# The opening of a three-layer stack: each entered group of channels feeds its chunk of three weight blocks instead of one

## The chip, the cores and the metric

One core of one Trainium2 chip runs the whole program. The metric is the device time of one execution in microseconds (us), taken as the median of the runs; lower is better.

## The reference, cut to what matters

Two hybrid layers and one further layer work on 256 tokens of 2048 channels. Only the start of the first layer is touched by the change:

```
mod = dot(silu(c), w_ada) + b_ada          # c: 2048; w_ada: 2048 x 6144
shift, scale, gate = split(mod, 3)
u = rms_norm(x, norm_w) * (1 + scale) + shift
proj = dot(u, w_in)                        # w_in: 2048 x 19064
... iq (index queries, 1024 columns), dk and dv (keys and values, 512),
    ik, iw, dt, f (128 columns, "misc"), dq (1024), and the rest
```

So the first product with w_in can start only when shift and scale are known for a group of channels, and these are themselves sums over 16 MB each of w_ada.

## The kernel before, in words

**Numbers.** All operands are f32. Every product with w_in is made of three products of rounded pieces: the weights are split into HH (ScalarE, `hi`, L1455) and LL (VectorE, `lo`, L1812, written in place over RAW), u into UH and UL. A *chunk* is 1 MB of weights: four k-tiles of 128 rows by 512 columns. With 256 tokens in two halves that is 24 matmuls of 128x512 (L1214), each `gemm`. Four chunks make a *block* of 512 output columns, which ends in two PSUM banks. Blocks alternate between two pairs of banks (`set`, G0/G1 and G2/G3).

**Order.** A planner (`Order`) writes one list of steps; each engine's program is the list's steps of its kind, in that order, with semaphores between engines. An engine thus never passes a step that waits. After each `gemm` comes a `slot`: one step of a lane `side` (attention, index scores, scan work, rope tables) and one of a lane `evac` (what follows a finished block). Lanes are first in, first out. All weights are fetched by the SP queue (L1069), in the order of the list, and each fetch first waits until the last reader of its buffer is done (L1066).

**The opening** (`open`, the first layer only). The 2048 channels enter in four groups of four 128-channel tiles. For one group, eight sums over the 2048 inputs of w_ada are needed: four for scale, four for shift. Each sum reads 1 MB. Six are made on VectorE (`dot`, L1805, one pass over 128x2048 with a running sum), two on TensorE (L1231, 16 products with one moving column, 32 matmuls in the trace; `ON_PE = 2`). The order in a group is: shift 2 on TensorE, scale 0 and 1, shift 3 on TensorE, scale 2 and 3, then the fetch and `hi` of the group's chunk of the first index query block, shift 0 and 1. Then `am` (L1897 to L1902) adds the biases, `u` scales and shifts the group's channels (ScalarE L1504 and L1509, VectorE L1954), and `lo` and `gemm` of that chunk follow directly. The sums use six fetch buffers in turn (0 to 5), the chunks two (6 and 7).

**The first x.** x is loaded, squared (ScalarE L1447), scaled by its root (L1468, two halves one after the other) and turned by TensorE through the banks BA and BC (L1246, L1459) within the first group.

**After the opening** one chunk is multiplied per slot: the last of iq0, then misc, iq1, dkv, dq0, dq1, the convolution blocks (from chunk 21 on) and so on. Five buffers serve them, and sums for the second layer (`ada`, 1 MB each, L1823) are woven in at two per five chunks until the convolution blocks. `misc_work` runs in seven slots once misc is done, and index scores, the first attention and the scan follow it on the side lane. In every block of heads (`heads`) the two token halves are copied, rotated and turned in slots of their own, through bank BE. The rope tables are side steps of the opening's slots.

Of the kernel before, what the change touches and what calls it, by code (L numbers as in the profile page):

```python
# [32 lines left out]

ON_PE = 2

# [69 lines left out]
class Order:  # L105
# [3 lines left out]
    def __init__(self):  # L109
        self.plan = []  # L110
        self.evac, self.side = Lane(), Lane()
        self.packed = {}
        dots = list(range(NR + NX - 2))

        self.ring, self.buf_user = {"dot_dve": dots, "dot_pe": dots, "all": [NR + NX - 2, NR + NX - 1]}, {}
        self.fetches = []
        self.chunks = []
        self.blocks = []
        self.pend = []
        self.evac_last, self.side_last = ("start",), ("start",)  # L120
        self.evac_before, self.side_before = {}, {}
        self.user = [None, None]
        self.ada = {"list": [], "i": 0, "job": None, "every": 0, "count": 0, "next": 0, "got": []}
        self.ada_info, self.cb, self.dots = [], [], {}
# [100 lines left out]
    def begin(self, chunks, evac, x, ready, kts, needs=None, after=None, soon=None):  # L225
        b = {"n": len(self.blocks), "set": len(self.blocks) % 2, "x": x, "ready": ready, "kts": kts, "evac": evac, "chunks": chunks,
             "needs": needs or (lambda k0: []), "after": after, "soon": soon, "job": None, "free_by": None, "end": None}
# [86 lines left out]

    def open(self, block, between, enter):


        for gi in range(4):
            dots = [("scale", m, "dve") for m in range(4)] + [("shift", m, "dve") for m in range(4 - ON_PE)]
            for i, m in zip((0, 3), range(4 - ON_PE, 4)):  # L320
                dots.insert(i, ("shift", m, "pe"))
            for i, (kind, m, engine) in enumerate(dots):
                if i == 6:
                    self.bring(block["chunks"][gi])
                self.dot(kind, 4 * gi + m, engine)
                between(gi, i)
            enter(gi)
            if gi < 3:
                self.put("lo", block["chunks"][gi]["g"])
                self.gemm(block["chunks"][gi])  # L330
                self.slot()
        self.pend.append(block["chunks"][3])
        self.ring = {"all": sorted(range(NR), key=lambda i: self.buf_user[i])}


def work_order():
# [23 lines left out]

    def heads(h):
        def steps(b):
            o.head_block[h] = b
# [122 lines left out]

    def enter_first(gi):
        put("am", 0, gi)
        put("u", 0, gi)
        ended("u_lo", 0, 2 * gi + 1)  # L490
# [32 lines left out]

    o.head_block, o.tok_block, o.freed = {}, {}, {}

# [122 lines left out]
    put("start")  # L648
    for gen in (load_layer(0), rope(0), rope(1)):
        o.side.add(gen)  # L650
# [4 lines left out]
    for l in range(2):  # L655
# [10 lines left out]
        if l == 0:  # L666
            first = o.wblock(w, IQ, heads(("iq", 0, 0)), u_ready, kind="tm", begun=True)
            o.open(first, first_x, enter_first)
            o.ada["list"] += [(1, part, pair, half) for half in range(2) for part in range(2) for pair in range(8)]
            o.ada["every"] = (2, 5)  # L670
            iq_b = [first]
        else:
            iq_b = [o.wblock(w, IQ, heads(("iq", l, 0)), u_ready, kind="tm", needs=u_needs, soon=(lambda e=entered: e))]
        misc_b = o.block([one], misc(l), ("U", 0), u_ready, KT)
        iq_b.append(o.wblock(w, IQ + 512, heads(("iq", l, 1)), u_ready, kind="tm"))
        o.side.add(o.when([misc_b], misc_work(l)))
        o.side.add(o.when(iq_b, index_scores(l)))
        dkv_b = o.wblock(w, DK, heads(("dk", l, 0)), u_ready, kind="tm")
        dq_b = [o.wblock(w, DQ + j * 512, heads(("dq", l, j)), u_ready, kind="tm") for j in range(2)]
# [84 lines left out]
def hybrid_stack(nc, A, out):  # L764
# [181 lines left out]
    x_turned, x_put = count("x_turned", o.all("x_in")), count("x_put", o.all("x_in"))  # L946
    x_sum, x_normed = count("x_sum", o.all("x_norm")), count("x_normed", o.all("x_norm"))
    rope_ang = count("rope_ang", o.all("rope"))
# [93 lines left out]
    def tokens_of(b, t):  # L1042

        return (gemm_done if t else tm_half).at(o.blocks[b]["last"])

    def freed(key):
# [131 lines left out]
    def tensor_program(pe):  # L1178
# [60 lines left out]
        def x_in(c):  # L1239
            bk = (BA, BC)[c % 2]  # L1240
            pe.wait_ge(*x_normed.at(1))
            if c >= 2:
# [32 lines left out]
        def hd_turn(h, t):  # L1275
            weight, rot, n = HEADS[h[0]]
            pe.wait_ge(*(hd_rot if rot else hd_scaled).at(h, t))
            pe.wait_ge(*(hd_put.at(h, 0) if t else evac_before("hd", h, 0)))
            for c in range(n):
                mm = pe.transpose(BE[:, c * P:(c + 1) * P], SS[t][:, c * P:(c + 1) * P], ident)  # L1280
            mm.then_inc(*hd_turned.up(h, t))
# [150 lines left out]
    def scalar_program(a):  # L1432
# [30 lines left out]

        def x_norm(t):
            a.wait_ge(*x_sum.at(t))
            rstd(0, t, SSQ[:, t:t + 1])
            a.wait_ge(*rstd_done.at(0, t))
            a.activation(kv2[:, t, :], kv2[:, t, :], ACT.Copy, scale=RST[:, t:t + 1]).then_inc(*x_normed.up(t))  # L1468

# [65 lines left out]
        def hd_store(h, t):  # L1535
            weight, rot, n = HEADS[h[0]]
            dst, first = head_dst[h[0]](h[2])
            scale = {"fq": PB[:, 120:121], "fk": PB[:, 121:122], "dq": HD_SCALE, "q2": HD_SCALE}
            a.wait_ge(*hd_turned.at(h, t))
            a.activation(dst[:, first:first + n, t * P:(t + 1) * P], BE[:, 0:n * P].rearrange("p (a b) -> p a b", a=n),  # L1540
                         ACT.Copy, scale=scale[h[0]] if h[0] in scale else 1.0).then_inc(*hd_put.up(h, t))
# [242 lines left out]
    def vector_program(v):  # L1784
# [96 lines left out]

        def x_norm(t):
            rstd(0, t)

# [595 lines left out]
```

## Time and profile before

| what | value |
|---|---|
| median of 3 runs | 3477.04 us (3476.33 to 3477.14) |
| profiled execution, its own time | 3473.09 us |
| its span | 3471.3 us |
| TensorE busy | 3335.0 us, 96% of the span |
| VectorE busy | 2238.9 us, 64% |
| ScalarE busy | 1701.7 us, 49% |
| moved by DMA | 719.32 MB, 207 GB/s over the span |

The profile is one execution. A busy engine is one whose instructions are running; TensorE's granted clock is given beside it in tenths of full speed or as a share. The trace is counted in us from the start of the span.

### The profile page before, as it was taken

How to read it: one execution, taken by the hardware profiler on the slowest of the kernel's cores; microseconds unless marked ns; L12 is line 12 of the kernel's file. 1: busy time of each engine (PE TensorE's matmuls, PEld its weight loads, DVE VectorE, ACT ScalarE, POOL GpSimd, SP SyncE). 2: the span in 40 equal slices, each digit the busy share in tenths (PEclk: the TensorE clock that was granted, in tenths of full speed). 3: DMA queues.
4: the chain of work that ended last, by engine and by line, in shares of the span. 5: the costliest groups of instructions: out<-in, count | busy, mean ns of one | idle time of the engine just before them, and what ended most of it. 6: DMA issues, size and time to landing. Idle time of an engine off the chain costs nothing.

```text
span 3471.3 us, 43913 instructions
## 1 busy us (share of the span) xinstructions
PE 3335.0 (96%) x18250; PEld 2894.8 (83%) x18250; DVE 2238.9 (64%) x2687; ACT 1701.7 (49%) x2098; POOL 46.8 (1%) x90
## 2 busy tenths in 40 slices
PE   5799989989999999999999999999999999999998
PEld 4679978878888887799788878888888899988887
DVE  5688777866666556687666576655567776544544
ACT  3354565554434344546655544343446875434343
POOL 0000000000000000000000000000000000000000
PEclk8799999999999999999999999999999999999999
DMA  8654456556677655444544467765555443455554
GB/s 354 261 222 173 170 209 248 219 199 249 260 279 287 224 183 193 162 179 158 180 172 159 174 234 267 272 249 196 189 183 191 177 173 140 158 218 194 194 184 156
DMA packets 102918, 719.32 MB, mean 207 GB/s; under 512 B 12176, under 2 KB 12256, under 8 KB 18752
## 3 DMA queue, kind: packets, MB, share of 16 engines
q1 hardware_dynamic: 93888, 675.38, 52.5%
q0 software_dynamic: 8256, 37.64, 3.1%
q8 instruction: 144, 2.36, 0.3%
q10 hardware_dynamic: 576, 3.50, 0.3%
q14 instruction: 54, 0.44, 0.0%
HBM read 710.08 MB, written 6.40 MB: 206 GB/s over the span
## 4 chain that ended last, share of the span: by engine, by line
PE 86%; DVE 7%; ACT 3%; DMA 2%; issue 1%; SPq 0%; DVEq 0%; ACTq 0%
PE G L1214 79%; DVE LL L1812 3%; DMA RAW<-w_ada_turned_packed_dram 1%; PE BA L1362 1%; PE BD L1335 1%; DVE S L2019 1%; PE BD L1397 1%; DMA RAW<-in_w_in_packed_dram 1%; ACT HH L1455 1%; PE BC L1348 0%; DVE RAW L1823 0%; PE BE L1280 0%; PE BA L1416 0%; PE BC L1416 0%; PE BC L1380 0%
## 5 line engine op out<-in xcount | busy, mean ns | idle before, releaser
L1455 ACT ACTIVATE HH<-RAW 128x2048 fp32r<-128x2048 f32 x546 | 1044.7, 1914 | 1138.1 <-PE G L1214 838.4
L1812 DVE TENSOR_TENSOR LL<-RAW,HH 128x2048 fp32r<-128x2048 f32 x546 | 1247.8, 2287 | 357.8 <-ACT HH L1455 357.3
L1214 PE MATMUL G<-HH,UH 128*128 128x512 f32 x2560 | 1022.1, 399 | 61.2 <-DVE LL L1812 57.2
L1214 PE MATMUL G<-LL,UH 128*128 128x512 f32 x2560 | 1003.6, 392 | 0.0
L1214 PE MATMUL G<-HH,UL 128*128 128x512 f32 x2560 | 1003.3, 392 | 0.0
L1214 PEld LDWEIGHTS G<-HH,UH 128*128 128x128 f32 x2560 | 485.1, 189 | 171.0 <-DVE LL L1812 67.4
L1214 PE MATMUL G<-UH,HH 128*128 128x256 f32 x2080 | 602.9, 290 | 9.8 <-DVE XS L2055 7.2
L1214 PE MATMUL G<-UH,LL 128*128 128x256 f32 x2080 | 589.2, 283 | 0.0
L1214 PE MATMUL G<-UL,HH 128*128 128x256 f32 x2080 | 588.9, 283 | 0.0
L1214 PEld LDWEIGHTS G<-LL,UH 128*128 128x128 f32 x2560 | 484.5, 189 | 103.7
L1214 PEld LDWEIGHTS G<-HH,UL 128*128 128x128 f32 x2560 | 485.6, 190 | 100.6 <-issue 2.9
L1214 PEld LDWEIGHTS G<-UH,HH 128*128 128x128 f32 x2080 | 399.4, 192 | 15.7 <-DVE LL L1812 12.5
L1214 PEld LDWEIGHTS G<-UL,HH 128*128 128x128 f32 x2080 | 399.5, 192 | 2.0 <-issue 1.0
L1214 PEld LDWEIGHTS G<-UH,LL 128*128 128x128 f32 x2080 | 399.1, 192 | 0.0
L1214 PE MATMUL G<-HH,YH 128*128 128x512 f32 x768 | 299.9, 391 | 3.0 <-DVE LL L1812 3.0
L1214 PE MATMUL G<-LL,YH 128*128 128x512 f32 x768 | 298.9, 389 | 0.0
L1214 PE MATMUL G<-HH,YL 128*128 128x512 f32 x768 | 298.8, 389 | 0.0
L1214 PEld LDWEIGHTS G<-HH,YH 128*128 128x128 f32 x768 | 144.2, 188 | 33.6 <-DVE LL L1812 3.9
L1214 PEld LDWEIGHTS G<-LL,YH 128*128 128x128 f32 x768 | 144.1, 188 | 30.3
L1214 PEld LDWEIGHTS G<-HH,YL 128*128 128x128 f32 x768 | 144.2, 188 | 29.4
L1823 DVE SCALAR_TENSOR_TENSOR RAW<-RAW,CH 128x1024 f32<-128x1024 f32 x128 | 151.4, 1220 | 11.5 <-DMA RAW<-w_ada_turned_packed_dram 11.5
L2019 DVE SCALAR_TENSOR_TENSOR S<-G,PAR,S 128x253 f32<-128x253 f32 x144 | 69.3, 481 | 52.1 <-ACT S L1571 48.3
(336 smaller groups left out, 2304.2 us busy)
## 6 DMA issues: line engine op xcount, KB each, us to landing
RAW<-in_w_in_packed_dram SPq DMA_DIRECT2D x402, 1024.0 KB, 4.8
RAW<-w_ada_turned_packed_dram SPq DMA_DIRECT2D x88, 1024.0 KB, 4.9
RAW<-in_w_out_packed_dram SPq DMA_DIRECT2D x48, 1024.0 KB, 4.8
RAW<-in_w_o_ssd_packed_dram SPq DMA_DIRECT2D x32, 1024.0 KB, 4.8
RAW<-in_w_o_fox_packed_dram SPq DMA_DIRECT2D x16, 1024.0 KB, 4.8
RAW<-in_w_o_dsa_packed_dram SPq DMA_DIRECT2D x16, 1024.0 KB, 4.9
RAW<-in_w_proj_a_packed_dram SPq DMA_DIRECT2D x16, 1024.0 KB, 4.8
RAW<-in_w_proj_b_packed_dram SPq DMA_DIRECT2D x16, 1024.0 KB, 4.8
```

The lines of the kernel that those rows point to most:

```text
L1214: mm = pe.matmul(to, lt, rh, start=first, stop=end, skip_group_check=True)
L1335: mm = pe.matmul(BD[:, j * P:(j + 1) * P], vt[:, t, vof(h + j):vof(h + j) + P], W[3][:, (j * nt + t) * P:(j * nt + t + 1) * P], start=t == ...
L1362: mm = pe.matmul(to, QQ[:, h + j, qt * P:(qt + 1) * P], kt[:, kof(h + j), 0:nk], start=True, stop=True)
L1397: pe.matmul(BD[:, j * 64:(j + 1) * 64], W[j // 4][:, (j % 4) * P:(j % 4 + 1) * P], XD[:, j * 64:(j + 1) * 64], start=True, stop=True)
L1455: a.activation(HH[g % NH][:, :n], RAW[buf(ch["f"])][:, :n], ACT.Copy).then_inc(*hi_done.up(g))
L1812: v.tensor_tensor(LL[buf(f)][:, :n], RAW[buf(f)][:, :n], HH[g % NH][:, :n].bitcast(F32), ALU.subtract).then_inc(*lo_done.up(g))
L1823: done = v.scalar_tensor_tensor(r, r, 0.5, CH[:, :], ALU.mult, ALU.mult, accum_out=DOT[:, e["half"], c:c + 1])
L2019: v.scalar_tensor_tensor(to, of, weight(j), to, ALU.mult, ALU.add).then_inc(*done.up(*key, n))
```

## The change

The opening now serves three blocks: both index query blocks and the keys and values. Each group of channels brings three chunks. In the order of a group, the chunks' fetches stand before shift 0, shift 1 and the TensorE sum; one sum is on TensorE and seven on VectorE. `u` and the three products of a group are no longer at its end but inside the next group: `u` and two chunks after scale 1, the third chunk after scale 3. The sums use four buffers (5, 6, 7, 0), the chunks four (1 to 4). The third block's sums are kept in the banks BA and BC. The first rope table is made ahead of the opening, x is normed earlier and with one semaphore, and the three blocks' heads are worked off with both token halves in one slot, turned through BE and BD. The misc block comes after the three.

```diff
-ON_PE = 2
+ON_PE = 1
+DOT_BUFS, CHUNK_BUFS = [5, 6, 7, 0], [1, 2, 3, 4]
...
-        dots = list(range(NR + NX - 2))
-        self.ring, self.buf_user = {"dot_dve": dots, "dot_pe": dots, "all": [NR + NX - 2, NR + NX - 1]}, {}
+        dots = list(DOT_BUFS)
+        self.ring, self.buf_user = {"dot_dve": dots, "dot_pe": dots, "all": list(CHUNK_BUFS)}, {}
...
-    def open(self, block, between, enter):
+    def open(self, blocks, between, am, u):
+        def chunk(gi, n):
+            return blocks[n]["chunks"][gi]
+        def multiply(gi, ns):
+            for n in ns:
+                self.put("lo", chunk(gi, n)["g"])
+                self.gemm(chunk(gi, n))
+                self.slot()
         for gi in range(4):
             dots = [("scale", m, "dve") for m in range(4)] + [("shift", m, "dve") for m in range(4 - ON_PE)]
-            for i, m in zip((0, 3), range(4 - ON_PE, 4)):
-                dots.insert(i, ("shift", m, "pe"))
+            for m in range(4 - ON_PE, 4):
+                dots.insert(6, ("shift", m, "pe"))
             for i, (kind, m, engine) in enumerate(dots):
-                if i == 6:
-                    self.bring(block["chunks"][gi])
+                if 4 <= i < 7:
+                    self.bring(chunk(gi, i - 4))
                 self.dot(kind, 4 * gi + m, engine)
                 between(gi, i)
-            enter(gi)
-            if gi < 3:
-                self.put("lo", block["chunks"][gi]["g"])
-                self.gemm(block["chunks"][gi])
-                self.slot()
-        self.pend.append(block["chunks"][3])
+                if gi and i == 1:
+                    u(gi - 1)
+                    multiply(gi - 1, (0, 1))
+                elif gi and i == 3:
+                    multiply(gi - 1, (2,))
+            am(gi)
+        u(3)
+        multiply(3, (0,))
+        self.put("lo", chunk(3, 1)["g"])
+        self.pend += [chunk(3, 1), chunk(3, 2)]
...
     def first_x(gi, i):
-        if gi == 0 and i == 4:
-            put("x_norm", 0)
-            put("x_norm", 1)
-        if gi == 0 and i == 5:
+        if gi == 0 and i == 1:
+            put("x_norm")
+        if gi == 0 and i == 3:
             for c in range(KT // 2):
                 put("x_in", c)
...
-    def heads(h):
+    def heads(h, two_banks=False):
+        def at_once(b):
+            o.head_block[h] = b
+            o.two_banks.add(h)
+            for t in range(2):
+                put("hd", h, t)
+            o.blocks[b]["free_by"] = ("hd_scaled" if HEADS[h[0]][0] else "hd_copied", h, 1)
+            yield
+            for t in range(2):
+                put("hd_turn", h, t)
+            ended("hd_put", h, 1)
...
     put("start")
-    for gen in (load_layer(0), rope(0), rope(1)):
+    for part in range(2):
+        put("rope", 0, part)
+    for gen in (load_layer(0), rope(1)):
         o.side.add(gen)
...
-            first = o.wblock(w, IQ, heads(("iq", 0, 0)), u_ready, kind="tm", begun=True)
-            o.open(first, first_x, enter_first)
+            iq_b = [o.wblock(w, IQ + j * 512, heads(("iq", 0, j), True), u_ready, kind="tm", begun=True) for j in range(2)]
+            dkv_b = o.wblock(w, DK, heads(("dk", 0, 0), True), u_ready, kind="tm", begun=True)
+            o.open(iq_b + [dkv_b], first_x, am_first, u_first)
...
+    GB.append([BA, BC])
```

## Rows read from the trace of the kernel before

**Rows 1.** Busy by stretch: PE, PEld, DVE, ACT, POOL, clock, DMA share, GB/s.

```profile
0.00:134.00 134.00, 74.38 (x360) 67.92 (x360) 76.76 (x103) 42.49 (x54) 3.56 (x10) 0.75 0.86 346
134.00:212.00 78.00, 74.36 (x342) 60.85 (x343) 58.07 (x101) 40.36 (x52) 1.09 (x2) 0.95 0.52 193
212.00:430.00 218.00, 215.69 (x1592) 201.73 (x1591) 171.41 (x300) 117.06 (x208) 1.10 (x2) 1.00 0.50 184
430.00:480.00 50.00, 41.06 (x180) 32.53 (x179) 31.85 (x42) 31.61 (x70) 1.06 (x2) 0.93 0.62 232
480.00:700.00 220.00, 216.79 (x1235) 187.74 (x1234) 172.42 (x233) 119.90 (x201) 3.17 (x6) 0.99 0.60 223
```

**Rows 2.** What the SP queue waited for, 0 to 150 us: total, times, longest.

```profile
SPq L1069 <- PE BE L1231: 48.0, 4, 20.2
SPq L1069 <- PE BD L1231: 42.9, 4, 17.7
```

**Rows 3.** Chain that ended last, 0 to 160 us: start, us, what.

```profile
57.01 4.09 PE BE L1231 x32
61.12 0.33 SPq L1069
61.49 7.07 DMA RAW<-w_ada_turned_packed_dram
68.58 2.31 DVE RAW L1805 x2
...
77.72 8.48 PE G L1214 x24
...
106.12 7.95 PE G L1214 x24
...
134.19 13.35 PE G L1214 x72
```

**Rows 4.** VectorE in order of time: start, us; waits in brackets.

```profile
16.47 2.29 DVE L1805 SCALAR_TENSOR_TENSOR RAW<-RAW,CB 128x2048 f32<-128x2048 f32 x1 [6.67 <-DMA RAW<-w_ada_turned_packed_dram]
...
66.06 2.29 DVE L1805 SCALAR_TENSOR_TENSOR RAW<-RAW,CB 128x2048 f32<-128x2048 f32 x1 [7.33 <-DMA RAW<-w_ada_turned_packed_dram]
...
106.71 0.26 DVE L1868 SCALAR_TENSOR_TENSOR WW<-WW 128x96 f32<-128x96 f32 x1
...
127.48 0.16 DVE L1897 TENSOR_TENSOR AM<-DOT,MOD 128x4 f32<-128x4 f32 x1
...
130.64 1.29 DVE L1954 TENSOR_TENSOR UL<-S,UH 128x512 fp32r<-128x512 f32 x2 [2.66 <-ACT UH L1509]
131.85 4.48 DVE L1812 TENSOR_TENSOR LL<-RAW,HH 128x2048 fp32r<-128x2048 f32 x2
...
141.73 2.29 DVE L1812 TENSOR_TENSOR LL<-RAW,HH 128x2048 fp32r<-128x2048 f32 x1
```

**Rows 5.** ScalarE in order of time, same columns.

```profile
19.28 1.91 ACT L1447 ACTIVATE XS<-KV 128x2048 f32<-128x2048 f32 x1 [0.69 <-DMA KV<-in_x_dram]
...
140.31 0.58 ACT L1533 ACTIVATE S<-G 128x512 f32<-128x512 f32 x1
...
199.17 1.92 ACT L1455 ACTIVATE HH<-RAW 128x2048 fp32r<-128x2048 f32 x1 [5.05 <-DMA RAW<-in_w_in_packed_dram]
201.11 1.28 ACT L1684 ACT_TABLE_LOAD   x1
```

**Rows 6.** TensorE in order of time: sums before warm-up and after.

```profile
25.38 6.99 PE L1231 MATMUL BD<-CT,RAW 128*128 128x1 f32 x32 [6.98 <-DMA RAW<-in_w_ada_packed_dram]
...
86.05 9.68 PE L1231 MATMUL BD<-CT,RAW 128*128 128x1 f32 x64
```

**Rows 7.** Chain that ended last, 180 to 235 us: start, us, what.

```profile
183.35 10.95 PE G L1214 x48
...
211.56 8.45 PE G L1214 x36
```

**Rows 8.** DMA rate in 40 equal slices of 0 to 134 us.

```profile
GB/s 147 393 259 432 408 418 418 423 423 421 421 423 423 421 423 418 86 0 120 423 406 320 423 421 428 279 5 318 423 421 428 430 426 372 2 198 423 399 374 428
```

More of the change, by code:

```diff
@@ L225, in begin @@
     def begin(self, chunks, evac, x, ready, kts, needs=None, after=None, soon=None):
-        b = {"n": len(self.blocks), "set": len(self.blocks) % 2, "x": x, "ready": ready, "kts": kts, "evac": evac, "chunks": chunks,
+        n = len(self.blocks)
+        b = {"n": n, "set": n if n < 3 else (n - 3) % 2, "x": x, "ready": ready, "kts": kts, "evac": evac, "chunks": chunks,
              "needs": needs or (lambda k0: []), "after": after, "soon": soon, "job": None, "free_by": None, "end": None}
@@ L359, in rope @@
         side_ended("rope_sin", r, 1)
-    def heads(h):
+    def heads(h, two_banks=False):
[9 more added lines that the diff above has]
+            ended("hd_put", h, 1)
         def steps(b):
+            if two_banks:
+                yield from at_once(b)
+                return
             o.head_block[h] = b
@@ L522, in out_layer @@
                 o.evac.add(modulated(l + 1))
-    o.head_block, o.tok_block, o.freed = {}, {}, {}
+    o.head_block, o.tok_block, o.freed, o.two_banks = {}, {}, {}, set()
     def load_layer(which):
@@ L666, in work_order @@
         if l == 0:
-            first = o.wblock(w, IQ, heads(("iq", 0, 0)), u_ready, kind="tm", begun=True)
-            o.open(first, first_x, enter_first)
+            iq_b = [o.wblock(w, IQ + j * 512, heads(("iq", 0, j), True), u_ready, kind="tm", begun=True) for j in range(2)]
+            dkv_b = o.wblock(w, DK, heads(("dk", 0, 0), True), u_ready, kind="tm", begun=True)
+            o.open(iq_b + [dkv_b], first_x, am_first, u_first)
             o.ada["list"] += [(1, part, pair, half) for half in range(2) for part in range(2) for pair in range(8)]
             o.ada["every"] = (2, 5)
-            iq_b = [first]
+            misc_b = o.block([one], misc(l), ("U", 0), u_ready, KT)
         else:
             iq_b = [o.wblock(w, IQ, heads(("iq", l, 0)), u_ready, kind="tm", needs=u_needs, soon=(lambda e=entered: e))]
-        misc_b = o.block([one], misc(l), ("U", 0), u_ready, KT)
-        iq_b.append(o.wblock(w, IQ + 512, heads(("iq", l, 1)), u_ready, kind="tm"))
+            misc_b = o.block([one], misc(l), ("U", 0), u_ready, KT)
+            iq_b.append(o.wblock(w, IQ + 512, heads(("iq", l, 1)), u_ready, kind="tm"))
         o.side.add(o.when([misc_b], misc_work(l)))
         o.side.add(o.when(iq_b, index_scores(l)))
-        dkv_b = o.wblock(w, DK, heads(("dk", l, 0)), u_ready, kind="tm")
+        if l:
+            dkv_b = o.wblock(w, DK, heads(("dk", l, 0)), u_ready, kind="tm")
         dq_b = [o.wblock(w, DQ + j * 512, heads(("dq", l, j)), u_ready, kind="tm") for j in range(2)]
@@ L1044, in tokens_of, with turn_bank @@
         return (gemm_done if t else tm_half).at(o.blocks[b]["last"])
+    def turn_bank(h, t):
+        return BD if t and h in o.two_banks else BE
     def freed(key):
@@ L1277, in hd_turn @@
             pe.wait_ge(*(hd_rot if rot else hd_scaled).at(h, t))
-            pe.wait_ge(*(hd_put.at(h, 0) if t else evac_before("hd", h, 0)))
+            pe.wait_ge(*(hd_put.at(h, 0) if t and h not in o.two_banks else evac_before("hd", h, 0)))
             for c in range(n):
-                mm = pe.transpose(BE[:, c * P:(c + 1) * P], SS[t][:, c * P:(c + 1) * P], ident)
+                mm = pe.transpose(turn_bank(h, t)[:, c * P:(c + 1) * P], SS[t][:, c * P:(c + 1) * P], ident)
             mm.then_inc(*hd_turned.up(h, t))
@@ L1462, in rstd, with x_norm @@
             a.activation(RST[:, t:t + 1], sq, ACT.Sqrt, bias=EPT[:, 0:1], scale=1.0 / D).then_inc(*rstd_root.up(n, t))
[L1464 to L1468, printed above, removed]
+        def x_norm():
+            for t in range(2):
+                a.wait_ge(*x_sum.at(t))
+                rstd(0, t, SSQ[:, t:t + 1])
+            for t in range(2):
+                a.wait_ge(*rstd_done.at(0, t))
+                i = a.activation(kv2[:, t, :], kv2[:, t, :], ACT.Copy, scale=RST[:, t:t + 1])
+            i.then_inc(*x_normed.up())
         def norm(n, t):
@@ L1880, in rstd, with x_norm @@
             v.reciprocal(RST[:, t:t + 1], RST[:, t:t + 1]).then_inc(*rstd_done.up(n, t))
-        def x_norm(t):
-            rstd(0, t)
+        def x_norm():
+            for t in range(2):
+                rstd(0, t)
         def norm(n, t):
```

12 lines of the change are left out of this document (7 added, 5 removed).

## The prediction, made before the changed kernel ran

> **What bounds the kernel now.** I read the busy time by stretch first. Outside the opening TensorE is all but full: 215.7 of 218 us between 212 and 430, 216.8 of 220 between 480 and 700. In the first 134 us it is busy 74.4, at a mean clock of 0.75, and most of that is not products with w_in [rows 1]. So a product that moves from behind the opening into its holes is won, as long as the opening does not grow by as much.
>
> Then what paces the opening. The SP queue waits 91 us for TensorE's sums, eight times [rows 2], and the DMA rate falls from about 421 GB/s to nothing once in each group [rows 8]. The chain shows one turn: a TensorE sum ends at 61.1, SP issues, a transfer lands, a VectorE sum ends at 70.9, ScalarE scales the channels, and the group's product starts at 77.7; the next two start at 106.1 and 134.2 [rows 3]. A turn is 28.2 us. Neither DMA nor VectorE fills it.
>
> **Prices.** 1 MB (1.049 MB in bytes) at 421 GB/s is 2.5 us [rows 8]. A fetch issued into an idle queue at 61.12 is used at 66.06, 4.9 us later, and the next at 68.56, 2.5 after it [rows 3, 4]. Two `lo` in sequence take 4.5 us, and a sum lasts as long, so each is 2.2 [rows 4]. A warm chunk is 10.95 / 2 = 5.5 us [rows 7]. A chunk after an idle stretch is 8.5 and 8.0 us, and less before shorter waits [rows 3]: I take 7.9. From `am` to the first product is 134.19 - 127.48 = 6.7 us [rows 3, 4]. A TensorE sum is 7.0 us at the 1.2 GHz level [rows 6] and 4.1 just after a chunk [rows 3].
>
> **What is removed and what is added.** At 134.19 the kernel before has nine chunks of these three blocks and misc still to multiply. After the changed opening only three and misc remain, so 6 x 5.5 = 33 us leave the full stretch. The opening gets eight more fetches, four more sums and six more `lo` steps on VectorE (22 us together), and four TensorE sums fewer, worth 16 to 28 us of PE time that lay under waits.
>
> If only the sum of work counted, a group would need 11 fetches x 2.5 = 27.4 us of DMA; VectorE 7 x 2.2 + 3 x 2.2 + 1.3 + 0.7 = 24; TensorE 7.9 + 11 + 4 = 23. All under the present 28.2. But the buffers join them into a ring. The four chunk buffers serve three chunks per group, so chunk 1 of group g goes where chunk 0 of group g-1 was, and chunk 2 where chunk 1 of g-1 was; the reader is the product. In SP's order the TensorE sum's and the last VectorE sum's fetches stand behind chunk 2. Hence this turn, from the end of product 1 of group g-1 (call it 0):
>
> chunk 2 issued 0, lands 4.9; TensorE sum's data 7.4; last VectorE sum's data 9.9; summed 12.2; `am` 12.9; two sums of the next group (they stand before `u` on VectorE, and cover the 2.7 that it now waits there for ScalarE [rows 4]) 17.3; UL 18.6; `lo` 20.8; product 0, cold, 28.7; product 1, 34.2.
>
> That is 34.2 us a turn in place of 28.2. The TensorE sum is covered: product 2 runs from 0 to 5.5, the sum from 7.4 to about 12, while VectorE waits until 12.2. If product 2 is late, or the sum runs at 7.0, it ends at 14.4 and `am` waits 2.2 more.
>
> **The first group.** The first rope table stands ahead of the first sum. Its second half waits for ScalarE, which first squares x until 21.3 [rows 5]; with a table load of 1.3 [rows 5], a sine of some 0.3 and five VectorE steps of 0.26 behind it [rows 4], the first sum starts at about 24.2 instead of 16.5 [rows 4]. It frees buffer 5 at 26.5, and the sixth fetch goes out then; five are in the queue, the fifth landing at about 27.9, so little of DMA is lost. From there each transfer follows at 2.5: shift 0 31.4, chunk 1 33.9, shift 1 36.4, chunk 2 38.9, TensorE's 41.4, the last 43.9; summed 46.2, `am` 46.9. The data of the next two sums land at 46.4 and 48.9 and end by 51.3; UL 52.6, `lo` 54.8. Product 0 54.9 to 62.8, product 1 to 68.3. x is ready before that: it is scaled right after the second sum (28.6), two passes of 2, and turned in 7, so by 40.
>
> Two turns more: 68.3 + 68.4 = 136.7. From there the fourth group's last sum ends 12.2 later (148.9), and 6.9 after that its first product starts: **155.8 us, against 134.2 before: 21.6 later**.
>
> **To the common point.** The two orders meet at the start of chunk 15 (third chunk of dq0), which before is 211.6, the product behind a stall [rows 7]. After: chunk 9 cold 7.9; then a new hole, because both halves of the first heads stand before `lo` of chunk 10 on VectorE and the second half can only be copied when chunk 9 is through: from the copy at 140.31 to the next `lo` at 141.73 it is 1.4 now [rows 4, 5], and with `lo` 2.2 and the handovers 3.8; chunks 10, 11, 13, 14 22; misc 5.8; turning heads 2.3. Together 41.8, so 197.6: 14 us earlier. The fetches are early enough, each buffer being freed some 12 us before its chunk is due.
>
> The 14 us hold something that may come back. Before 211.6, TensorE waits 10 us: a chunk lands at 199.2, after ScalarE waited 5.1 for it, and behind its `hi` come the misc chain, three table loads and the second half of the keys' heads [rows 5, 7]. In the new order misc follows eight chunks later, among the first convolution blocks, where no `ada` fetches hold up the ring (the 5 us for the landing chunk), but the chain is the same. Ends: nothing and 10 us. I take 5, for the half that was not the landing. So 9 us are left.
>
> The side lane behind it (index scores, first attention) moves by eight slots too. Convolution blocks carry it at 99% of TensorE [rows 1], so losing it there wins nothing; on the head blocks it meets square roots. These blocks lose 3.2 us in 220 when the scan shares them, but 8.9 in 50 where its first unit meets two halves of heads [rows 1]. The first unit of the scan moves off the first head block, so I set this at zero, between -6 and +18. The `ada` sums that drop out of the shortened stretch (about three) move to later blocks where TensorE is full and VectorE has room: nothing. The changed bank sets and semaphores of x: nothing, under the same waits.
>
> **Sum.** +21.6 for the opening, -35.6 from there to chunk 15 (77.4 becomes 41.8), +5: **-9 us**. Against the profiled execution, 3471.3 of span and 3473.1 of time, that is 3462 and 3464; the median lies 3.9 above that time, so 3468.
>
> One rule speaks to the DMA price. The Trainium skill, "DMA: Bandwidth & Descriptors", section "Where 436 GB/s comes from", holds that loads from HBM are bound by about 358 GB/s per core, not by the fabric's 435. [Rows 8] show 418 to 430 GB/s for tens of us, so the measurement decides against it here. By the rule, 1 MB would be 2.9 us, a turn would be 35.1 and the opening some 3 us longer, an estimate from that page.
>
> **The rivals.**
>
> A, the forecast: the turn is paced by the two products that free the chunk buffers. -9, with 3460 to 3475 as its own range. Half.
>
> B, DMA paces the groups: if the product's end is early enough, a group is 27.4 us, 6.8 less in each of two turns, -9 - 14 = -23, so 3454. For it: DMA runs unbroken whenever SP is free [rows 8]. Against it: SP must wait for the product by its own order. 0.15.
>
> C, no change to be measured: the misc stall comes back whole (+5) and the TensorE sum runs at the lower level in each group, 2.2 x 3 = +6.6, since those sums let the clock fall even now (9.7 us for two [rows 6]). +3, so 3480; with one of them alone 3473 to 3475. 0.2.
>
> D, slower: the first attention lands on the four halves of the fq heads. ScalarE changes its table for each, at 1.28 [rows 5], and TensorE waits as between 430 and 480, 8.9 us for two halves [rows 1]: 18 for four, -9 + 18 = +9, so 3486. It decides for slower from 16 us on. Against it: the scan does the same beside the fk heads and little is lost. 0.15.
>
> **How the numbers follow.** 0.2%, 7 us, is what can be told from no change. Of A's half, 0.36 falls beyond 7 us and 0.14 within; B adds 0.15 to faster, C 0.2 to the same, D 0.15 to slower. Faster 0.51, same 0.34, slower 0.15. The range takes in A, B and C and the lower edge of D: 3454 to 3484.
>
> **What would show it.** Right: the first products of the four groups' chunk 0 start at about 55, 89, 123 and 156; SP waits for L1214, not for L1231; a product's end, then an issue, in the chain; TensorE idle some 10 us per group before product 0, and the clock low at its start; a hole of about 4 us after chunk 9; chunk 15 near 198. Wrong: a start of the fourth group at 142 (B); TensorE's sum as the last to end before `am` (C); idle time on TensorE between 380 and 480 above that of before (D). The prediction falls if the opening is off by more than 6 us, or if holes behind chunk 15 are more than 10 us larger or smaller.

## The result and the profile after

| | before | changed |
|---|---|---|
| median of the runs | 3476.68 us (4 runs, 3471.77 to 3477.14) | 3453.69 us (4 runs, 3453.29 to 3454.94) |
| span of the profiled execution | 3471.3 us | 3451.8 us |
| TensorE busy | 3335.0 us | 3314.4 us |

The ratio is 0.9939, with a 95% interval from 0.9927 to 0.995. By the medians the kernel became 23 us faster (17 to 25 by the interval); 9 had been forecast. The first line of the changed kernel's page:

```profile
PE 3314.4 (96%) x18122; PEld 2876.5 (83%) x18122; DVE 2248.8 (65%) x2695; ACT 1698.0 (49%) x2096; POOL 46.8 (1%) x90
```

**The opening after.** The chain of the changed kernel (start, us, what), which answers to [rows 3]:

```profile
56.66 13.42 PE G L1255 x48
70.10 0.33 SPq L1110
70.47 6.86 DMA RAW<-in_w_ada_packed_dram
77.38 5.96 PE BE L1272 x32
83.71 4.42 DVE RAW L1850 x4
...
91.59 13.06 PE G L1255 x48
...
126.66 12.64 PE G L1255 x48
139.32 0.33 SPq L1110
139.70 8.49 DMA RAW<-in_w_ada_packed_dram
148.23 7.00 PE BE L1272 x32
...
161.82 8.28 PE G L1255 x24
...
173.90 7.37 PE G L1255 x24
```

L1255 is the product (L1214 before) and L1272 the sum on TensorE. The groups' first products start at 56.7, 91.6, 126.7 and 161.8; about 55, 89, 123 and 156 had been forecast. Each turn is two products, the issue that their end allows, a transfer, and then TensorE's own sum. SyncE's waits from 0 to 150 (waited for, us, times, longest), which answer to [rows 2]:

```profile
SPq L1110 <- PE G L1255: 52.6, 6, 13.3
SPq L1110 <- DVE RAW L1850: 42.7, 12, 22.0
SPq L1110 <- PE BD L1272: 18.3, 2, 9.3
SPq L1110 <- PE BE L1272: 6.6, 1, 6.6
```

The queue that waited 91 us for TensorE's sums now waits 25 for them and 53 for the products. VectorE's timeline in the last group (start, us, instruction, idle before and its releaser) shows the sum ending last:

```profile
155.26 0.16 DVE L1946 TENSOR_TENSOR SH<-BE,MOD 128x1 f32<-128x1 f32 x1 [1.89 <-PE BE L1272]
```

**By stretch.** Columns as in [rows 1]; the changed kernel:

```profile
0.00:162.00 162.00, 88.33 (x377) 75.65 (x378) 104.64 (x135) 56.47 (x63) 3.56 (x10) 0.78 0.80 319
162.00:194.00 32.00, 28.19 (x136) 23.76 (x137) 16.11 (x24) 8.92 (x10) 0.00 (x0) 0.86 0.36 129
194.00:212.00 18.00, 18.00 (x84) 14.91 (x83) 10.32 (x23) 10.73 (x21) 0.00 (x0) 1.00 0.66 238
212.00:430.00 218.00, 214.30 (x1567) 199.95 (x1567) 180.45 (x318) 122.78 (x221) 2.20 (x4) 1.00 0.50 180
430.00:480.00 50.00, 46.61 (x234) 38.15 (x233) 34.27 (x43) 32.75 (x65) 0.53 (x1) 1.00 0.58 219
```

To 194, TensorE is idle for 73.7 and 3.8 us, 77.5 in all; from 194 to 212 not at all. In the next two it is idle for 3.7 and 3.4 us. It was 2.3 and 8.9 in the kernel before [rows 1], where the second is the stretch with the scan's first unit and two halves of heads: rival D's collision did not come.

**A fairer common point.** Chunk 15, which the prediction used, is not preceded by the same work in both kernels, and as it turned out the stall ahead of it was misread. The start of chunk 13 is cleaner: both kernels have then multiplied the three blocks and misc. It is 194.12 before and 194.01 after. In 194 us the opening and its three blocks have won 0.1. The same view of the kernel before, around that point:

```profile
134.19:194.20 60.01, 60.00 (x285) 49.76 (x286) 45.52 (x71) 29.82 (x35) 0.00 (x0) 0.97 0.52 195
194.20:211.56 17.36, 13.92 (x57) 10.69 (x55) 11.93 (x27) 9.91 (x17) 1.09 (x2) 0.90 0.49 185
```

Where the starts of some later chunks lie (us), and what each stretch gave:

| start of | before | changed | won in the stretch |
|---|---|---|---|
| chunk 13 | 194.12 | 194.01 | 0.1 |
| convolution blocks (21) | 251.80 | 240.06 | 11.6 |
| fq blocks | 411.32 | 399.34 | 0.2 |
| gates behind fv | 582.65 | 565.15 | 5.5 |
| sz blocks | 635.95 | 619.64 | -1.2 |
| second gates | 753.18 | 731.61 | 5.3 |
| third branch product | 860.91 | 840.07 | -0.7 |
| end of the span | 3471.3 | 3451.8 | -1.3 |

The table's 11.6 is in part TensorE work of the side lane that now comes after the start of the convolution blocks (run 8 shows it), so a single row is rough; the sum is not. So 19.4 of the 19.5 us lie behind the point at which the changed part of the program is over. Idle time says the same. Before chunk 13 TensorE is idle 59.8 us before (134.19 less the 74.4 busy of [rows 1], and nothing from there) and 77.5 after: 17.7 more. Its busy time there shrank by about as much, from 134.3 to 116.5, since half of its sums are gone. Over the whole span idle time grew by only 1.1 (3471.3 less 3335.0 is 136.3, and 3451.8 less 3314.4 is 137.4), so behind that point 16.6 us of holes have closed. The two stretches in which most closed, of the kernel before and then of the changed one:

```profile
411.32:582.65 171.33, 158.71 (x734) 128.53 (x732) 128.05 (x160) 100.01 (x190) 3.71 (x7) 0.97 0.59 224
635.95:753.18 117.23, 105.44 (x502) 87.18 (x501) 84.93 (x120) 67.36 (x95) 0.00 (x0) 0.95 0.58 215
```

```profile
399.34:565.15 165.81, 161.63 (x799) 133.55 (x798) 129.30 (x172) 105.47 (x215) 3.18 (x6) 1.00 0.61 227
619.64:731.61 111.97, 104.47 (x515) 87.00 (x513) 90.06 (x136) 69.27 (x103) 0.00 (x0) 1.00 0.59 216
```

Idle there: 12.6 and 11.8 before, 4.2 and 7.5 after; 3.4 more closed from 194.20 to 211.56, 16.1 together. The same blocks are multiplied in these stretches. They became 5.5 and 5.3 us shorter. The first won less than its idle time lost, since TensorE also does more in it (799 matmuls for 734, 2.9 us): work of the side lane has moved there. TensorE's waits in the first of them, before and then after:

```profile
PE G L1214 <- DVE LL L1812: 6.1, 5, 1.5
PE BE L1280 <- DVE S L1976: 5.7, 3, 3.0
```

```profile
PE G L1255 <- DVE LL L1857: 2.6, 2, 1.5
```

L1280 turns a half of heads and waits for VectorE's rotation or scaling of it. Those waits are gone.

### The profile page after: what moved, and what is told of

It is laid out like the page before. It is cut to its first block, busy times and chain, and to the rows that moved or that the text cites. A ratio compares the mean times of both kernels' runs of the same rounds, so it can differ in the third digit from the quotient of the medians.

```text
span 3451.8 us, 43659 instructions
## 1 busy us (share of the span) xinstructions
PE 3314.4 (96%) x18122; PEld 2876.5 (83%) x18122; DVE 2248.8 (65%) x2695; ACT 1698.0 (49%) x2096; POOL 46.8 (1%) x90
## 4 chain that ended last, share of the span: by engine, by line
PE 86%; DVE 8%; ACT 3%; DMA 2%; issue 1%; DVEq 0%; ACTq 0%; SPq 0%
PE G L1255 79%; DVE LL L1857 3%; DMA RAW<-in_w_ada_packed_dram 1%; PE BA L1403 1%; PE BD L1376 1%; PE BD L1438 1%; DVE S L2065 1%; ACT HH L1496 1%; DVE RAW L1850 1%; DVE RAW L1868 1%; DMA KV<-in_x_dram 0%; PE BC L1389 0%; PE BA L1457 0%; PE BC L1457 0%; PE BD L1272 0%
## 5 line engine op out<-in xcount | busy, mean ns | idle before, releaser
L1255 PE MATMUL G<-HH,UH 128*128 128x512 f32 x2528 | 1006.1, 398 | 48.8 <-DVE LL L1857 44.2
L1255 PE MATMUL G<-LL,UH 128*128 128x512 f32 x2528 | 989.0, 391 | 0.0
L1255 PE MATMUL G<-HH,UL 128*128 128x512 f32 x2528 | 988.7, 391 | 0.0
L1255 PE MATMUL G<-UH,HH 128*128 128x256 f32 x2080 | 604.5, 291 | 12.1 <-DVE XS L2101 8.2
L1255 PEld LDWEIGHTS G<-HH,UH 128*128 128x128 f32 x2528 | 477.7, 189 | 154.4 <-DVE LL L1857 52.2
L1255 PE MATMUL G<-UH,LL 128*128 128x256 f32 x2080 | 590.6, 284 | 0.0
L1255 PE MATMUL G<-UL,HH 128*128 128x256 f32 x2080 | 590.6, 284 | 0.0
L1255 PEld LDWEIGHTS G<-LL,UH 128*128 128x128 f32 x2528 | 477.2, 189 | 101.5
L1255 PEld LDWEIGHTS G<-HH,UL 128*128 128x128 f32 x2528 | 477.9, 189 | 98.6 <-issue 2.6
L1255 PEld LDWEIGHTS G<-UH,HH 128*128 128x128 f32 x2080 | 400.9, 193 | 19.5 <-DVE LL L1857 15.0
L1255 PEld LDWEIGHTS G<-UL,HH 128*128 128x128 f32 x2080 | 401.2, 193 | 2.1 <-issue 1.2
L1255 PEld LDWEIGHTS G<-UH,LL 128*128 128x128 f32 x2080 | 400.9, 193 | 0.0
L1255 PE MATMUL G<-HH,YH 128*128 128x512 f32 x768 | 300.6, 391 | 2.8 <-DVE LL L1857 2.8
L1255 PE MATMUL G<-LL,YH 128*128 128x512 f32 x768 | 299.6, 390 | 0.0
L1255 PE MATMUL G<-HH,YL 128*128 128x512 f32 x768 | 299.5, 390 | 0.0
L1255 PEld LDWEIGHTS G<-HH,YH 128*128 128x128 f32 x768 | 144.6, 188 | 33.6 <-DVE LL L1857 3.7
L1255 PEld LDWEIGHTS G<-LL,YH 128*128 128x128 f32 x768 | 144.6, 188 | 30.2
L1255 PEld LDWEIGHTS G<-HH,YL 128*128 128x128 f32 x768 | 144.5, 188 | 29.7
```

Source lines behind the costliest of these rows:

```text
L1255: mm = pe.matmul(to, lt, rh, start=first, stop=end, skip_group_check=True)
```

## The experiments: the opening

Every kernel here computes the whole reference. Ratios are to the kernel before on the same chip. The intervals of runs 1 to 5 overlap with that of the changed kernel (0.9927 to 0.995), so of these runs the starts in the trace, one execution each, say more than the medians; that of run 6 does not overlap.

**1. Five chunk buffers.** If the products pace a turn by freeing the chunk buffers, a fifth buffer shortens it; if DMA paces it, it does not.

```diff
-DOT_BUFS, CHUNK_BUFS = [5, 6, 7, 0], [1, 2, 3, 4]
+DOT_BUFS, CHUNK_BUFS = [5, 6, 7], [0, 1, 2, 3, 4]
```

> The changed kernel with five buffers for chunks and three for sums, in place of four and four. Theory (the turn of 35 us is paced by the end of product 1 of the group before, which frees the buffer of chunk 2): chunk 2 now waits for product 0 only, 5.5 us earlier, but the second sum of the next group then waits for TensorE's sum, so a turn is 31 to 33 us and the fourth group's first product starts at 153 to 158 in place of 161.8. Rival 1 (the DMA engines have no more to give): the turn stays at 35. Rival 2 (TensorE's sum paces the turn): with three sum buffers it gets longer, 36 or more. Time: 4 to 8 us less by the theory, none or more by the rivals.

Median 3451.89, ratio 0.9933 (0.9918 to 0.9948). The first and the last of the groups' first products in the chain (the others start at 97.6 and 130.9):

```profile
63.87 12.89 PE G L1255 x48
...
160.10 7.15 PE G L1255 x24
```

The turns are 33.7, 33.4 and 29.2 in place of 34.9, 35.1 and 35.2. They are shorter, but the first two do not reach the 31 to 33 expected. In the chain a turn now holds all three products of a group, TensorE's sum right behind them (4.34 and 4.12 us) and a transfer for the next group's sum, which waited for that sum's buffer. The first group starts 7.2 later, and its chain too goes through TensorE's sum, whose end frees a buffer for a later sum. At 160.1 the fourth group is past the 153 to 158 expected. The price of the first group was missing from the expectation, and the whole, 1.8 us by the medians against 4 to 8 expected, is no gain that can be told from none.

**2. Chunk 2's fetch behind the last sum's.** The fetches of TensorE's and the last VectorE sum no longer stand behind the one that waits for the second product.

```diff
-                if 4 <= i < 7:
+                if 4 <= i < 6:
                     self.bring(chunk(gi, i - 4))
                 self.dot(kind, 4 * gi + m, engine)
+                if i == 7:
+                    self.bring(chunk(gi, 2))
```

> The changed kernel with the third chunk of a group fetched behind all of the group's sums. Theory (the end of product 1 paces the turn through SP's order): the sums' data no longer wait for product 1, but the next group's two sums now stand behind chunk 2, which does; the turn shrinks by 1 to 2 us only, fourth group's product at 156 to 159, time 3 to 6 us less. Rival (TensorE's sum and its data are what ends last): the turn shrinks by the whole 3 to 5 us, fourth group's product at 147 to 152, time 9 to 15 us less.

Median 3449.51, ratio 0.9927 (0.9912 to 0.9941).

```profile
123.71 13.52 PE G L1257 x48
137.24 10.59 DMA RAW<-in_w_in_packed_dram
...
155.82 7.43 PE G L1257 x24
```

The fourth group starts at 155.8, 6 us earlier, about as expected (156 to 159). It is not 1 to 2 us a turn, though: the first group is 2.2 earlier, and the turns are 34.2, 35.1 and 32.1, so the rest came nearly all in the last. What ends the last turn is now the chunk's transfer.

**3. All eight sums on VectorE.** This asks what TensorE's own sum costs.

```diff
-ON_PE = 1
+ON_PE = 0
...
-            v.wait_ge(*dot_pe.at("shift", c + 3))
-            v.tensor_tensor(SH[:, e:c + 4], pe_part[:, e - c:4], MOD[:, e:c + 4], ALU.add).then_inc(*own.up())
+            if ON_PE:
+                v.wait_ge(*dot_pe.at("shift", c + 3))
+                v.tensor_tensor(SH[:, e:c + 4], pe_part[:, e - c:4], MOD[:, e:c + 4], ALU.add).then_inc(*own.up())
```

> The changed kernel with the last TensorE sum of each group on VectorE too (nothing on TensorE). Theory (TensorE's sum, at half rate behind idle stretches, adds only the 0.7 to 1.9 us by which VectorE now waits for it in each group): fourth group's product at 156 to 158 in place of 161.8, time 4 to 6 us less. Rival (the sum on TensorE is free, VectorE's 2.2 us more per group is on the path): 162 to 170, time the same or up to 8 us more.

Median 3447.14, ratio 0.992 (0.9903 to 0.9937).

```profile
156.41 7.08 PE G L1255 x24
```

The groups start at 54.5, 89.8, 124.2 and 156.4: 5.4 us earlier in the fourth, 6.5 in the median. VectorE, which was busy 104.6 of 162 us in the changed kernel, takes the eighth sum without loss; TensorE's was on the path.

**4. `lo` of chunk 10 ahead of the first heads.** The hole behind chunk 9 is put down to the two halves of heads that stand before it on VectorE.

```diff
         u(3)
-        multiply(3, (0,))
+        self.put("lo", chunk(3, 0)["g"])
         self.put("lo", chunk(3, 1)["g"])
+        self.gemm(chunk(3, 0))
+        self.slot()
```

> The changed kernel with the low piece of chunk 10 made before the heads of the first block, not after them. Theory (the 3.8 us hole behind chunk 9 is a wait of VectorE for the heads' second half, and the chunk after it runs 1.9 us long at the lower clock): both go, 5 to 6 us less at the start of the convolution blocks (240.1 now), and in the time. Rival (what is won here is given back at later holes): the same at the convolution blocks, but 0 to 2 us less at the end.

Median 3447.37, ratio 0.992 (0.9905 to 0.9935).

```profile
162.27 14.07 PE G L1257 x48
```

The hole is gone (14.07 for both chunks, where the changed kernel needs 8.28 + 3.80 + 7.37), and the convolution blocks start 4.9 us earlier. The slow second chunk was a part of the hole's price.

**5. Two blocks served.** The number of products in a turn is the theory's main term. Here the keys and values keep their old way.

```diff
-                if 4 <= i < 7:
+                if 4 <= i < 6:
                     self.bring(chunk(gi, i - 4))
...
-                    multiply(gi - 1, (0, 1))
+                    multiply(gi - 1, (0,))
                 elif gi and i == 3:
-                    multiply(gi - 1, (2,))
+                    multiply(gi - 1, (1,))
...
-            o.open(iq_b + [dkv_b], first_x, am_first, u_first)
+            o.open(iq_b, first_x, am_first, u_first)
...
+            dkv_b = o.wblock(w, DK, heads(("dk", 0, 0), True), u_ready, kind="tm")
```

> The changed kernel with two blocks served in the opening (both of the index queries), keys and values behind it. With four chunk buffers and two chunks a group, no fetch waits for a product of the group before. Theory (the turn of 35 us is paced by that wait): a turn of 26 to 29 us and the fourth group's first product at 138 to 145 in place of 161.8, but three more chunks behind it and one saved hole less: the start of the convolution blocks at 236 to 243 (240.1 now), so the same time within 5 us. Rival (the turn is paced by TensorE's sum and ScalarE, whatever the buffers): a turn of 33 to 35, convolution blocks at 252 to 256, time 12 to 16 us more.

Median 3457.0, ratio 0.9948 (0.9931 to 0.9964). SyncE's waits from 0 to 160:

```profile
SPq L1109 <- DVE RAW L1849: 81.5, 22, 22.4
SPq L1109 <- PE G L1254: 36.8, 4, 17.8
```

The turns are 28.5, 27.7 and 23.4, and the fourth group starts at 132.8, earlier than the 138 to 145 expected. SyncE now waits longest in total for VectorE's sums. Chunk 13's start, by the same work, is 181.5: 12.5 earlier than with three blocks. Yet the whole is 3.3 slower than the changed kernel by the medians and 1.8 by the profiled spans. At the start of the convolution blocks (234.3 against 240.1) 6.7 of the 12.5 are gone already, and behind them the stretch of fq to fv is 167.59 long, that of sz 114.56. An opening that was 12.5 us better lost all of it behind it. After this the question was the order behind the opening.

**6. The three repairs together** (2, 3 and 4 in one kernel, their diffs as above).

> The changed kernel with three edits that won alone: third chunk last in its group, all sums on VectorE, low piece of chunk 10 ahead of the heads. At the start of the convolution blocks they won 5.7, 5.6 and 5.0 us alone. Theory (the first two both shorten the last turn and overlap there; the third is independent): 11 to 14 us less at the convolution blocks and 10 to 13 less time. Rival (all three shorten one and the same wait): no more than 7.

Median 3438.25, ratio 0.9894 (0.9879 to 0.9908), 15.4 below the changed kernel. In the chain:

```profile
134.78 9.40 DMA RAW<-in_w_in_packed_dram
...
152.19 13.49 PE G L1259 x48
```

The repairs nearly add up: the fourth group starts 9.6 earlier, where 2 and 3 alone gave 6.0 and 5.4. Chunk 13 starts at 178.41 and the convolution blocks at 224.48, both 15.6 earlier, a little over the 11 to 14 expected; the time, too, is better than the 10 to 13. The later stretches are those of the changed kernel (165.95 and 111.96), so the gain arrives whole. This version is faster than both kernels.

**7. The first rope table behind two sums** (on top of 6).

```diff
     put("start")
-    for part in range(2):
-        put("rope", 0, part)
...
         if gi == 0 and i == 1:
+            for part in range(2):
+                put("rope", 0, part)
             put("x_norm")
```

> The three edits together (g_three_together) and the first rope table made behind the first two sums in place of ahead of them, so that the first sum need not wait until 24.1 for ScalarE. Theory (the DMA engines are full in the first group whatever VectorE does, 2.5 us for each transfer): the first product starts 1 to 2 us earlier (54.5 now), time 0 to 2 us less. Rival (the first group waits for VectorE): 5 to 8 us less.

Median 3438.06, ratio 0.9898 (0.9884 to 0.9911). The first product starts 1.25 earlier (53.24), and nothing of it is left later. The table ahead of the opening costs nothing that lasts: the transfers fill the time, as the prediction had it.

## The experiments: the order behind it

**8. The block order alone**, with the opening of before: both iq blocks, keys and values, then misc.

```diff
-            iq_b = [first]
+            iq_b = [first, o.wblock(w, IQ + 512, heads(("iq", l, 1)), u_ready, kind="tm")]
+            dkv_b = o.wblock(w, DK, heads(("dk", l, 0)), u_ready, kind="tm")
+            misc_b = o.block([one], misc(l), ("U", 0), u_ready, KT)
```

> The kernel before, with its own opening, and only the order of the blocks changed: iq0, iq1, keys and values, misc, then dq0 (misc eight chunks later, and with it the side lane: index scores, first attention, scan, second attention). Theory (the 8 us that the changed kernel wins behind the start of the convolution blocks come from that shift: its work meets other blocks): convolution blocks start at 251 to 253 as before (251.8), the first product of the branch blocks 5 to 8 us earlier than 825.2, time 5 to 8 us less. Rival (they come from the later sums of the second layer, or from the two-bank heads): 0 to 2 us.

Median 3467.44 against 3475.25, ratio 0.9977 (0.9968 to 0.9987): 7.8 us of the 23, in the 5 to 8 expected. The start of the convolution blocks came at 238.8, where 251 to 253 had been expected: TensorE's work of the side lane moves across that start, which so is no common point. The hole before 211.56 is gone, and idle time falls in the later stretches. They are no shorter than before (171.33 and 117.23), since TensorE is busy longer in them; the lead of 10.9 us at the start of the fq blocks becomes 7.2 at the end.

```profile
400.39:572.33 171.94, 163.15 (x788) 134.02 (x786) 128.07 (x171) 103.37 (x209) 3.69 (x7) 0.98 0.60 221
628.01:745.68 117.67, 107.72 (x514) 89.21 (x513) 90.14 (x135) 69.05 (x103) 0.00 (x0) 0.96 0.58 215
```

**9. Fewer `ada` fetches early**, one in five chunks instead of two until the dq blocks; before's order and opening.

```diff
-            o.ada["every"] = (2, 5)
+            o.ada["every"] = (1, 5)
             iq_b = [first]
```

> The kernel before, with the second layer's sums woven in at one per five chunks, not two, ahead of the convolution blocks: three there in place of six, as many as in the changed kernel, and the others later. Theory (the shift of the side lane makes the win): 0 to 2 us less. Rival (fewer of these fetches in the first stretch, or their other places later, make the win): 5 to 8 us less.

Median 3474.69, ratio 0.9997 (0.9988 to 1.0007): no effect. In this order of blocks their number early on is not the cause.

**10. Old opening, new tail.** The opening is that of before; the block order, the `ada` sums' places and the side lane's slots are those of the changed kernel, so that from chunk 24 on both lists of steps are the same.

```diff
     def misc_work(l):
+        if l == 0:
+            yield
         put("misc_pe", l)
...
-            iq_b = [first]
+            o.ada["every"] = 0
+            iq_b = [first, o.wblock(w, IQ + 512, heads(("iq", l, 1)), u_ready, kind="tm")]
+            dkv_b = o.wblock(w, DK, heads(("dk", l, 0)), u_ready, kind="tm")
+            o.ada["every"] = (2, 5)
+            misc_b = o.block([one], misc(l), ("U", 0), u_ready, KT)
```

> The kernel before with its own opening (one block served), and from chunk 24 on exactly the changed kernel's list of steps: block order iq0, iq1, keys and values, misc, no sums of the second layer before misc, and the misc work one slot later. The two openings have come to the same point (thirteen chunks and misc multiplied, chunk 13 started) at 192.9 with the block order alone and 194.0 in the changed kernel. Theory A (the whole win lies in the list behind the opening, the three-block opening itself gives nothing): within 2 us of the changed kernel, about 3450 to 3453 of span, 22 to 25 us less than before. Theory B (the three-block opening sets better starting conditions, buffers and lanes, for what follows): no better than with the block order alone, 3462 to 3466 of span, 7 to 10 us less than before.

Median 3451.22 against 3473.98, ratio 0.9935 (0.9923 to 0.9948): 22.8 us, the whole gain, without the new opening. Its chain has the old turns, and its later stretches are the changed kernel's to 0.1 us:

```profile
105.51 7.29 PE G L1221 x24
...
133.15 12.58 PE G L1221 x48
```

```profile
397.14:562.96 165.82, 161.62 (x799) 133.54 (x798) 129.35 (x172) 105.66 (x215) 3.17 (x6) 1.00 0.61 227
617.45:729.37 111.92, 104.43 (x515) 86.99 (x513) 90.14 (x136) 69.10 (x103) 0.00 (x0) 1.00 0.59 216
```

**11. The same, the side lane one slot earlier** (10 without the `yield` in `misc_work`).

> As h_old_opening_new_tail, but the misc work and all behind it on the side lane one slot earlier (as with the block order alone); the places of the second layer's sums as in the changed kernel. Theory A1 (the places of the second layer's sums against the heads and the scan make the rest of the win): within 2 us of h_old_opening_new_tail. Theory A2 (the one slot of the side lane makes it): within 2 us of the block order alone, some 12 us more than the other.

Median 3460.18, ratio 0.9955 (0.9939 to 0.997). Between 8 and 10 in ratio, and 9.0 us above 10 by the medians, on the same chip. The two intervals overlap, but of the single times only one of its four, 3454.17, lies within those of 10. Not all of that is the slot's. The stretch of fq to fv is even shorter (163.09, idle 3.0) and that of sz 0.4 longer; the loss is scattered: 2.3 us by chunk 13, 2.1 more by the fq blocks, 2.2 between the gates and sz, 1.7 between the second gates and the third branch, 3.4 behind its product. The first 2.3 are there when misc starts (187.94 against 185.59), and up to there TensorE does the same work in the same order in both kernels, so the slot has no part in them. From misc to the third branch product 3.6 us are left.

**12. The same as 10, the `ada` sums at the old places** of the fq to sz blocks (chunks 45, 47, 50, 52 and so on instead of 44, 47, 49, 52).

```diff
         o.ada["every"] = (2, 5) if l == 0 else 0
+        o.ada["count"] += 2
         fx_b = [o.wblock(w, FQ + j * 512, heads(("fq", l, j)), u_ready, kind="tm") for j in range(2)]
```

> As h_old_opening_new_tail, with the second layer's sums put one chunk off behind the convolution blocks: at chunks 45, 47, 50, 52, 55 and so on, where the kernel before has them, in place of 44, 47, 49, 52, 54. Their number up to there stays at three. Theory (their places against the two halves of the heads decide how long TensorE waits): the stretch of the fq and fk heads and fv takes 171 to 173 us as with the block order alone, in place of 165.8, the stretch of the sz blocks 116 to 118 in place of 111.9, and the time is 8 to 13 us more than h_old_opening_new_tail. Rival (fewer of them ahead of the convolution blocks is what counts, or the slot of the side lane): within 3 us of h_old_opening_new_tail.

Median 3458.78, ratio 0.9951 (0.9938 to 0.9965); some 5.5 us above 10 by the ratios, and the interval overlaps with that of 10.

```profile
398.98:567.90 168.92, 164.03 (x800) 135.60 (x798) 130.17 (x173) 105.05 (x215) 3.17 (x6) 0.98 0.60 223
622.38:736.93 114.55, 105.17 (x515) 87.25 (x513) 90.19 (x136) 69.19 (x103) 0.00 (x0) 0.98 0.60 220
```

Both stretches are about 3 us longer and the clock is again at 0.98, but not as long as the 171 to 173 and 116 to 118 expected. The places show in these stretches and are not all: of the 5.7 us, 3.0 come back before the third branch product. At misc this execution is 1.9 behind that of run 10, again ahead of any difference in the lists; from misc to the third branch product it loses 2.7. In TensorE's waits of the first stretch, the turn of a half of heads waits for VectorE three times before (5.7 us), once in 8 (3.4), once here (2.3), and never in the three kernels with the new places (changed, 10 and 11):

```profile
PE BE L1288 <- DVE S L1984: 2.3, 1, 2.3
```

Idle time of TensorE in the two stretches, from the rows above:

| kernel | fq to fv | sz |
|---|---|---|
| before: old opening, order and places | 12.6 | 11.8 |
| 8: new block order, old places | 8.8 | 10.0 |
| 12: new order and lane slots, old places | 4.9 | 9.4 |
| 10: new order, slots and places | 4.2 | 7.5 |
| changed | 4.2 | 7.5 |

## Why the prediction was right and where it was wrong

**Right in direction, off in size, and the direction by luck**: -9 forecast, -23 measured, just under the lower end of the range. The forecast gain was to come from products moved into the opening. By chunk 13 these gave 0.1, and run 10 has the whole gain without them. The time is also that of rival B (3454), by coincidence: B wanted the fourth group at 142, and it started at 161.8.

**The opening: mechanism right, size 6 us short.** "34.2 us a turn" was 34.9 to 35.2, and "155.8 us, against 134.2 before: 21.6 later" was 161.8, 27.6 later. Of the 6: the first group is 1.8 late; the rest is in the turns, and most of both is the term that was left to rival C. "The TensorE sum is covered" is the step that failed. In every group the sum ended last ahead of `am`: `am` waited 1.89, 0.85, 0.71 and 1.89 us for it, 5.3 in all. In the first and the last group it ran at the lower level (granted clock 0.50), 7.00 us for the 4.1 of one just after a chunk [rows 3]. Run 3 showed its price, 5.4; run 2, which lets its data come earlier, the same 6; both with 4 made 15.6. That products pace the ring (and not DMA, rival B) was borne out by SyncE's waits, by run 1's shorter turns and by run 5's 28; in run 1 TensorE's sum stands in the turn beside them.

**The hole behind chunk 9** was 3.80 as forecast (3.8). The chunk behind it ran cold too, 7.37 for 5.5, which the sum of 41.8 did not hold.

**"Before 211.6, TensorE waits 10 us" was false.** The wait of 10.1 for `lo`, in the answer for 134 to 215, is the idle time *ahead of the first product at 134.19*. The first line is from TensorE's waits, the second from its timeline:

```profile
PE G L1214 <- DVE LL L1812: 11.0, 2, 10.1
134.19 0.79 PE L1214 MATMUL G<-HH,UH 128*128 128x512 f32 x1 [10.10 <-DVE LL L1812]
```

Inside, TensorE was busy for 60.00 of 60.01 us up to 194.20, and idle 3.4 from there to 211.56. Nothing large could come back there, and the +5 was a price for nothing. Measured by chunk 15 the changed kernel is 6.2 us ahead (205.36 to 211.56), where 14 were forecast before the +5: the opening took 6.0 of the difference, and 43.5 us in place of 41.8 behind it the rest. By chunk 13 it is 0.1 ahead.

**What was set at zero was nearly everything.** "I set this at zero, between -6 and +18" was -13.3 by the prediction's own point, chunk 15 (19.5 less 6.2), and -19.4 from chunk 13. The prediction had the place: side lane and `ada` sums moving by eight slots against the head blocks. It judged the stretch by an average (TensorE 99% busy there) and priced hardly anything but losses. The 12.6 and 11.8 us of holes in the fq to fv and sz stretches were in the trace all along, and 12.7 of these 24.4 closed. Rival D, the first attention colliding with the fq heads, did not occur: the same stretch of fq to fv lost 8.4 us of idle time.

**Shown and not shown.** Shown: the old opening with the new tail gives the whole gain (10), so the three-block opening as built is worth nothing here (with the new order the old one comes to chunk 13 at 191.5 to 193.8 in the profiles of runs 8 and 10 to 12, the new one at 194.0), and repaired it is worth 15 more (6). Shown: the block order alone gives a third (8). Shown in part: the kernel with the side lane one slot earlier is 9.0 us slower (11) and that with the old `ada` places some 5.5 (12, whose interval overlaps with that of 10), but between misc and the third branch product only 3.6 and 2.7 us of it are seen in one profile each. Open: the rest, and why single slots are worth that. The stretches are located and one kind of wait (the turn of heads for VectorE) follows the places, but the rest of the program behind 840 us varies too, from 2610.2 to 2618.2 between single executions of the kernels of runs 10 to 12, and part of the differences of 11 and 12 is in it. Whether another slot is better still was not tried.

## What to carry to other kernels

When an edit at one end of a fixed order shifts everything behind it, compare first at a point where both kernels have done exactly the same work, and then run the old part with the new order behind it: here it was the whole gain. A cyclic pattern (two extra sums in five chunks, one side step a slot) meets the blocks' own steps at places that such a shift changes, so look for the holes that exist downstream and price both signs. And a wait listed for a window may belong to the idle time before an instruction at the window's first microsecond; ask for the busy time inside before calling it a stall.

## What the hardware showed that I had not expected

A sum on TensorE with one moving column is fast here only right behind a product. Of 32 matmuls each, in run 1 the last three took 3.72 to 4.34 us with no gap behind the product, at a mean granted clock of 0.78 to 0.91; in the changed kernel they took 5.96 to 7.00 after waits for their data, at 0.50 to 0.60. 7.00 to 3.72 is near the ratio of the two levels.

What follows an idle stretch pays again. In the changed kernel the chunk after a hole of only 3.8 us took 7.37 instead of 5.5 us, at a mean granted clock of 0.77, behind a chunk that had itself started at the lower level (8.28, at 0.67). A hole's price here was so 3.8 + 1.9, and run 4 got 4.9 of it back. In the stretches of fq to fv and of sz the mean granted clock rose from 0.97 and 0.95 to 1.00 as the holes closed.
